# One wide expert body with the choice of passes inside its blocks, first gates ahead of the dispatch, both tiles scattered by the next expert

## The reference, cut to what matters

```python
logits = (h @ w_router).astype(jnp.float32)
top_vals, top_idx = lax.top_k(logits, TOP_K)
gates = jax.nn.softmax(top_vals, axis=-1)
...
for e in range(N_EXPERTS):
    # swiglu: gu = h @ w_gu[e]; (silu(gu[..., :FF]) * gu[..., FF:]) @ w_down[e]
    y = y + comb[..., e:e + 1] * swiglu(h, w_gu[e], w_down[e])
return rmsnorm(h + y, final_norm_g)
```

## Time and profile before

| | |
|---|---|
| median of 3 runs | 1764.01 us (1763.48 to 1765.18) |
| the profiled execution | 1751.77 us, of which the span is 1750.0 us |
| granted TensorE clock, mean | 0.970 |
| busy share of the span: TensorE / its weight loads / VectorE / ScalarE / GpSimd | 93% / 75% / 72% / 58% / 7% |
| chain that ended last, by engine | PE 69%, DVE 11%, DMA 11%, ACT 4%, issue 4% |

### The profile page before, as it was taken

The page is one execution under the profiler, slowest core; times in us unless marked ns, Lnnn a source line. Parts: engine busy times, 40 slices in busy tenths (PEclk is TensorE's granted clock), DMA queues, the critical chain, the costliest instruction groups (busy, mean ns, idle before and its releaser), DMA issues.

```text
span 1750.0 us, 20830 instructions
## 1 busy us (share of the span) xinstructions
PE 1621.6 (93%) x7345; PEld 1318.3 (75%) x7346; DVE 1257.8 (72%) x1028; ACT 1022.6 (58%) x872; POOL 120.9 (7%) x90
## 2 busy tenths in 40 slices
PE   7999999999899769999999999999999599899996
PEld 5887778888788657777778878778888377677775
DVE  6745554544579559999988888655554499899996
ACT  4344344344348337887877777544443378788874
POOL 0000000000000003030030030020000030200300
PEclk9999999999999869999999999999999799999998
DMA  9652545555542118999999989846565299999994
GB/s 356 200 194 96 181 159 190 192 180 193 174 151 73 48 50 330 394 391 389 395 361 382 344 328 368 298 168 204 204 210 198 84 347 396 341 388 395 379 395 180
DMA packets 191591, 450.82 MB, mean 258 GB/s; under 512 B 8492, under 2 KB 8892, under 8 KB 191420
## 3 DMA queue, kind: packets, MB, share of 16 engines
q1 hardware_dynamic: 189212, 445.35, 70.2%
q10 hardware_dynamic: 2336, 4.85, 0.8%
HBM read 449.13 MB, written 1.05 MB: 257 GB/s over the span
## 4 chain that ended last, share of the span: by engine, by line
PE 69%; DVE 11%; DMA 11%; ACT 4%; issue 4%; SPq 0%; DVEq 0%; ACTq 0%; POOL 0%; POOLq 0%
PE bank L1148 19%; PE bank L1149 18%; PE bank L1152 18%; DMA raw<-in_moe_w_down 10%; DVE wlo L701 6%; ACT whi L406 4%; PE bank L1155 3%; PE bank L1156 3%; DVE y L939 2%; PE bank L1426 1%; PE bank L1425 1%; PE bank L1323 1%; PE bank L1325 1%; PE bank L1441 1%; PE bank L1442 1%
## 5 line engine op out<-in xcount | busy, mean ns | idle before, releaser
L701 DVE TENSOR_TENSOR wlo<-raw,whi 128x2048 fp32r<-128x2048 f32 x422 | 963.3, 2292 | 301.5 <-ACT whi L406 300.3
L406 ACT ACTIVATE whi<-raw 128x2048 fp32r<-128x2048 f32 x422 | 805.1, 1915 | 426.3 <-PE bank L1152 343.9
L1148 PE MATMUL bank<-whi,xx 128*128 128x512 f32 x1184 | 473.8, 400 | 47.3 <-issue 22.9
L1149 PE MATMUL bank<-wlo,xx 128*128 128x512 f32 x1184 | 466.0, 394 | 0.0
L1152 PE MATMUL bank<-whi,xx 128*128 128x512 f32 x1184 | 465.7, 393 | 0.0
L1148 PEld LDWEIGHTS bank<-whi,xx 128*128 128x128 f32 x1184 | 225.5, 190 | 97.3 <-issue 30.3
L1152 PEld LDWEIGHTS bank<-whi,xx 128*128 128x128 f32 x1184 | 225.3, 190 | 48.4
L1149 PEld LDWEIGHTS bank<-wlo,xx 128*128 128x128 f32 x1184 | 226.0, 191 | 45.3
L375 POOL TENSOR_SCALAR onehot<-mats,slot 128x64 fp32r<-128x64 f32 x64 | 110.3, 1747 | 921.6 <-PE bank L1432 921.6
L1155 PE MATMUL bank<-whi,hT 128*128 128x512 f32 x336 | 138.7, 413 | 23.8 <-DVE wlo L701 23.2
L1155 PE MATMUL bank<-whi,xx 128*128 128x512 f32 x336 | 133.6, 398 | 0.2
(11 more groups left out here) (201 smaller groups left out, 1298.6 us busy)
## 6 DMA issues: line engine op xcount, KB each, us to landing
raw<-in_moe_w_gu SPq DMA_DIRECT2D x224, 1024.0 KB, 7.7
raw<-in_moe_w_down SPq DMA_DIRECT2D x112, 1024.0 KB, 8.1
raw<-in_ffn_w_gu SPq DMA_DIRECT2D x28, 1024.0 KB, 5.0
raw<-in_ret_w_in SPq DMA_DIRECT2D x24, 1024.0 KB, 6.0
raw<-in_ffn_w_down SPq DMA_DIRECT2D x14, 1024.0 KB, 4.7
raw<-in_conv_w_pw SPq DMA_DIRECT2D x12, 1024.0 KB, 5.1
raw<-in_ret_w_out SPq DMA_DIRECT2D x8, 1024.0 KB, 4.7
res<-in_x SPq DMA_DIRECT2D x2, 512.0 KB, 5.3
```

Of the source, the lines that this page charges most:

```text
L406: nc.scalar.activation(whi[base % SPLIT][:, :], raw[base % RAW][:, :], ACT.Copy).then_inc(hi_done, 1)
L701: nc.vector.tensor_tensor(wlo[base % SPLIT][:, :], raw[base % RAW][:, :], whi[base % SPLIT][:, :].bitcast(f32), ALU.subtract).then_inc(lo_ ...
L1148: nc.tensor.matmul(dst, ah, bh, start=start, stop=False)
L1149: last = nc.tensor.matmul(dst, ah, bl, start=False, stop=stop and al is None)
```

## The change

- **Dispatch.** TensorE's loop computes tile 0's first two gate blocks ahead of the branch (`gates_first(0)`). The bodies are laid out as kind 0, kind 1, and one wide body for kinds 2 and 3; the four static ones become three.
- **Choice inside the wide body.** Each up block, down block and transposition does tile 0, and then branches on `need > 2` for tile 1: 35 such choices in a wide expert (2 + 1 ahead of the loop, 5 in each of 6 iterations, 2 behind it).
- **`pe_done`** of the first two gate blocks is raised by 2 at once: in a narrow body by a matmul of four columns with zeros (`nothing`) behind the branch, in the wide body behind tile 1's gates.
- **Wide entry.** Tile 0's gates no longer wait for tile 1: it has its own `xel2_done`. The order is gates of tile 0, branch, gather of tile 1, scatter of the previous expert, gates of tile 1. ScalarE's `hi` of the second block moves ahead of `xh_gathered2`, VectorE's `xl_gathered2` behind `y_lo`.
- **Wide exit.** The body's own scatter, `accumulate2` and both waits go. The next expert's `scatter_before` (in all three bodies and behind the loop) reads the previous expert's need and scatters one tile or two into the same banks, so that one `accumulate` adds both.

```diff
-            dve.wait_ge(moe_set, 4)
+            dve.wait_ge(moe_set, 5)
...
-            def xl_gathered(e, tiles, n):
+            def xl_gathered(e):
...
+            def xl_gathered2(n):
+                dve.wait_ge(xeh2_done, n + 1)
...
+                last.then_inc(xel2_done, 1)
...
-                xl_gathered(e, tiles, n2)
+                xl_gathered(e)
                 lo(B_MOE + 1, six)
                 y_lo(e)
+                if tiles == 2:
+                    xl_gathered2(n2)
...
                 if tiles == 2:
                     y_lo2(n2)
-                    accumulate2(e, n2)
...
+            def nothing(dst):
+                return nc.tensor.matmul(dst[:, 0:4], zeros[:, 0:P], zeros[:, 0:4], start=False, stop=True)
+
+            def expert_columns(base, acc, half, kind, need, six):
                 pe.wait_ge(lo_done, base + 1 + 6 * six)
+                if kind == WIDE:
+                    chunk_columns(base, acc[0], half, 0, FULL)
+                    with pe.If(need > 2):
+                        chunk_columns(base, acc[1], half, 1, FULL).then_inc(pe_done, 1)
+                    with pe.Else():
+                        chunk_columns(base, acc[1], half, 1, HALF_FULL).then_inc(pe_done, 1)
+                else:
+                    chunk_columns(base, acc[0], half, 0, kind).then_inc(pe_done, 1)
...
+            def scatter(tiles):
+                for t in range(TILES):
+                    for s in range(tiles):
...
+            def scatter_before(e):
+                pe.wait_ge(yl_done, e + 1)
+                with pe.If(need_before(pe, e) > 1):
+                    pe.wait_ge(y2l_done, wide_before(pe, e))
+                    scatter(2)
+                with pe.Else():
+                    scatter(1)
...
-            def expert(e, kinds):
...
-                pe.wait_ge(xel_done, e + 1)
-                columns(B_MOE, bank[0:2], 0, kinds=gates, six=six)
-                columns(B_MOE + 1, bank[0:2], 1, kinds=gates, six=six)
-                pe.wait_ge(yl_done, e + 1)
-                scatter(0, SCAT).then_inc(scat_ps, 1)
+            def expert(e, kind, need):
+                six, done, tiles = STEPS * e, STEPS * e + STEPS, 2 if kind == WIDE else 1
+                gates_end = nothing(bank[0])
+                if kind == WIDE:
+                    gather(e, 1).then_inc(gather2_ps, 1)
+                    scatter_before(e)
+                    pe.wait_ge(xel2_done, wide_before(pe, e) + 1)
+                    gates_first(1, six).then_inc(pe_done, 2)
+                else:
+                    gates_end.then_inc(pe_done, 2)
+                    scatter_before(e)
...
-                if tiles == 2:
-                    pe.wait_ge(y2l_done, n2 + 1)
-                    scatter(1, SCAT2).then_inc(scat2_ps, 1)
-                    pe.wait_ge(acc2_done, n2 + 1)
...
                 need = need_of(pe, e)
+                pe.wait_ge(xel_done, e + 1)
+                gates_first(0, STEPS * e)
+                with pe.If(need < 1):
+                    expert(e, HALF_FULL, need)
+                with pe.Else():
+                    with pe.If(need < 2):
+                        expert(e, FULL, need)
                     with pe.Else():
+                        expert(e, WIDE, need)
-            pe.wait_ge(yl_done, NE + 1)
-            scatter(0, SCAT).then_inc(scat_ps, 1)
+            scatter_before(NE)
```

More of the change, by code:

```diff
@@ L36 @@
 PAD = TAPS - 1
-FULL, HALF_FULL = 1, 2
+FULL, HALF_FULL, WIDE = 1, 2, 3
 MOE_BLOCKS = STEPS * STEP_BLOCKS
@@ new lines, in chunk_rows @@
+            def chunk_rows(base, first_chunk, stop, t, kind):
+                slot_ = base % SPLIT
+                for c in range(2):
+                    kc = first_chunk + c
+                    for n in range(2):
+                        col = c * D + n * BANK
+                        wh, wl = whi[slot_][:, col:col + BANK], wlo[slot_][:, col:col + BANK]
+                        dst = DOWN[t][n][:, :]
+                        if kind == HALF_FULL:
+                            last = half_product(dst, hTmix[:, kc, t, :], wh, wl, False, stop and c == 1)
+                        else:
+                            last = product(dst, hTh[:, kc, t, :], hTl[:, kc, t, :], wh, wl, False, stop and c == 1)
+                return last
@@ new lines, in scatter, with gates_first @@
+                last.then_inc(scat_ps, 1)
+            def scatter_before(e):
[3 more added lines that the diff above has]
+                    scatter(2)
+                with pe.Else():
+                    scatter(1)
+            def gates_first(tile, six):
+                for half in range(2):
+                    pe.wait_ge(lo_done, B_MOE + half + 1 + 6 * six)
+                    slot_ = (B_MOE + half) % SPLIT
+                    for c in range(4):
+                        kc = 4 * half + c
+                        last = product(bank[tile][:, :], xh[:, kc, tile, :], xl[:, kc, tile, :],
+                                       whi[slot_][:, c * BANK:(c + 1) * BANK], wlo[slot_][:, c * BANK:(c + 1) * BANK],
+                                       kc == 0, tile == 1 and kc == DC - 1)
+                return last
```

167 lines of the change are left out of this document (77 added, 90 removed).

## The result

The changed kernel takes **1737.48 us** (median of 4 runs, 1735.81 to 1740.53), beside 1763.74 us for the kernel before (4 runs): ratio 0.9854, interval 0.9842 to 0.9867. It gained 26.3 us; 10.9 were forecast, and 1753 us.

The account below looks back on a forecast made before the run. VectorE was taken to pace kind-0 stretches and TensorE the wide one, with code fetches at boundaries. Terms summed to -10.9 us, -16 of it at the wide exit: 1764.0 to 1753 us, range 1742 to 1763.

Parts of the forecast that it names:

- the same step: From profiled execution to median: the 12.2 us by which the median lay above it carried over unchanged, giving 1753 us.
- Leaving the wide expert: Wide expert's end to the next `hidden`: wait, scatter and `accumulate2` removed, fetch covered; -16 us (bounds -17 and -11).
- Expert 6: Start after the wide expert: its existing fetch stall stays, 0; -5.6 us if the smaller program stays at hand.
- Where a body ends: Start of expert 1: jump to the loop's end, code that never ran, costs a fetch; +5.6 us (bounds 0 and 5.6).
- Expert 3: Late `pe_done` there is hidden, since the chain ends where TensorE's up blocks end anyway: 0.
- `pe_done` late: Narrow experts: block 3's split waits for the late signal, delaying `hidden`; +1.2 us each for experts 1, 6 and 7.
- Wide entry: Entering the wide expert: full-clock gates and no fetch, but a new wait before the scatter; -3.5 us (bounds -6.3 and 0).
- The choices: The 35 branches in the wide body: 0.03 us each, +1 us in all (bounds 0 and 5).
- Expert 0: Its gates can start when `xx` is ready, partly offset by late `pe_done` and clock; -2.6 us (bounds -2.6 and 0).
- The first: Rival: all code stays at hand, no fetch at the starts of experts 1 and 6; 1742 us, chance 0.26.
- The second: Rival: late `pe_done` and body fetches at several narrow starts take the gain back; around 1764 us, chance 0.12.
- The third: Rival: the choices in the wide body drain TensorE, 0.6 us each; 1773 us, slower, chance 0.10.

Follow-up runs that it names:

- fourth look: One more profiled execution of the kernel before, unchanged: 1764.33 us.
- first look: The profiled execution of the kernel before, unchanged, on which the prediction was made: 1751.77 us.
- own_scatter: The changed kernel, but the wide expert again scatters its own tile 1 and waits, and `scatter_before` reads no table: 1740.01 us.
- narrow_first: The kernel before with only its four bodies reordered to kind 0, 1, 3, 2: 1753.4 us, ratio 0.9952.
- wide_first: The changed kernel with the wide body first, then kind 1 and kind 0: 1743.48 us.
- gates_in_bodies: The changed kernel with the first gates back in the bodies and `pe_done` raised by each block: 1743.36 us.
- one_narrow: The changed kernel with its two narrow bodies merged into one that chooses between the passes of kinds 0 and 1 inside its blocks: 1749.94 us.
- hinted: early_inc plus a branch hint on the back-edge of TensorE's expert loop: 1733.24 us, ratio 0.9837.
- early_inc: The changed kernel with `pe_done` raised once behind the first gate block of narrow experts: 1737.81 us.
- wide_first_hinted: wide_first plus the early `pe_done` increment in narrow experts and the hint on TensorE's expert loop back-edge: 1736.53 us.
- one_narrow_hinted: one_narrow plus the early `pe_done` increment in narrow experts and the hint on TensorE's expert loop back-edge: 1748.19 us.

## Why the prediction was wrong

**The step that failed** is the last: "The median is 12.2 above that execution; the same step puts the prediction at" 1753. It carries the offset over as if the change couldn't touch it. After has none (1737.84 profiled, 1737.48 median). The 26.3 us are 13.9 between the profiles, 12.0 of before's offset (1763.74 - 1751.77), and 0.4 of after's. Most of the offset (8.1 us by the fourth look) was late code at experts 5 to 7, with the clock behind it, and after has no such stall at 6 and 7; the rest was clock in an uncommonly fast first look. The sum itself, -10.9, missed the 13.9 by only 3, and that is partly luck: expert 6 came out 5.5 us shorter than forecast, and expert 3 came out 3.1 us longer. The fourth look is the execution to compare with; against it, after's stretches differ by -3.1 (up to expert 0), +6.8 (1), -0.2 (2), +1.5 (3), -4.8 (4), -17.5 (5), -5.5 (6), -4.4 (7) and +0.5 at the end: -26.5. Beside the forecast of -10.9, experts 6 and 7 make up 12.3 of the 15.6 us that are missing (+1.2 was forecast for each).

**Leaving the wide expert.** Forecast -16, between the profiles -16.2, and in the parts foreseen: input 6.4 us after the last product (1373.01 + 1.28 against 1367.85; 6.6 forecast), gates 6.6 after it, no fetch in the open. I had priced the whole, and not how it splits; 12.3 of it came in *own_scatter*, without moving the scatter.

**Expert 6.** This is the term of the sum that failed. I kept its stall at 0, with -5.6 as a bound "if the smaller program stays at hand". It went: -4.3 between the profiles, -5.5 with the late `pe_done` in it against the fourth look. With expert 7's stall, unseen in the first profile, that is the unforeseen part.

**Where a body ends.** Expert 1: forecast 5.6 + 1.2, measured 6.77, and *narrow_first* shows the cause alone (6.7 there without the late `pe_done`, and with more time at the low clock, so the match to a tenth is luck). **Expert 3**: forecast 0, measured +3.1. It jumps to the loop's end as expert 1 does, and I had that fetched once and for all. In *wide_first* the stall is gone with the order. Its stretch is 1.6 us longer than before's all the same, but before's own fourth look has that too (127.9), by the clock.

**`pe_done` late**: forecast 1.2, measured 1.3 at expert 7 and 1.1 by *gates_in_bodies*.

**Wide entry**: forecast -3.5, measured -3.0. The gather follows the gates without a gap, as foreseen. The wait is 4.49 us and not 3.9, and ends in "issue" 1.1 us after `yl` (1147.03 + 1.29): no instruction packet moves in it. It is the table read and the branch of `scatter_before`: *own_scatter*, which has neither, waits 3.48 us, and `yl` releases it. So an "issue" ending alone doesn't show a late instruction stream, and expert 0 showed the reverse, late code under another name; the packets have to be looked at. The read was left out of the sum here and put at +1 for the last scatter, where the wait did grow from 2.50 to 3.47 us; the last stretch, whose clock varies, went from 117.76 to only 117.87. The term of 2.8 for the clock has no row: the gates of the earlier trace rows take 7.5 instead of 5.5 us, which is 2.0.

**The choices**: forecast +1, measured 0 in the wide loop. **Expert 0**: forecast -2.6, measured -1.2 between the profiles, or -2.0 from the stage's own start, which came 0.8 us later. The size is near, the reason isn't: what stood before the gates was the fetch of the body. In *narrow_first*, with the gates in the body and the kind-0 body right behind the dispatch, it is gone; in *wide_first*, with the gates ahead and the wide body behind the dispatch, it stands behind the gates (2.45 and 2.91 us).

**The rivals.** The first, with all code at hand at 1742, was nearest in time, but not what happened: expert 1 stalls, expert 6 doesn't. The second was right in that one more narrow start stalls (expert 3), and wrong at the exit (-16.2, not -11) and at the wide entry (-3.0, not 0). The third fell with the step of the wide loop, 30.47 to 30.49 us with and without choices.

**Size or order.** Size alone doesn't rank the kernels: 1,660 instructions took 1750 us, 1,550 took 1725.5, and 1,840 took 1737.5 or, in another order, 1743.5. With the other edits and the body order left as before, it does: 2,360, 1,780 and 1,550 instructions give 1763, 1737.5 and 1725.5 us. The Trainium skill's page "Runtime: NRT & Kernel Launch", section "Instruction fetch mechanics", gives TensorE 128 KiB in blocks of 256 instructions; an estimate by it puts *one_narrow*'s stage at 104 KiB, all of it at hand once run, and the trace with its fetch at expert 2 disagrees. Which blocks are kept, and so where a layout stalls, no run here settles. One rival is untested: every edit that changes size or order also shifts where the code lies within its blocks, and no run shifted it alone.

## What to carry to other kernels

Code of a branchy stage is a resource: merging two bodies by a branch inside their blocks took 21 to 23 us off without touching the executed work, because a boundary that jumps to code not at hand costs 2 to 5.3 us of idle TensorE in these traces and 2 to 7.5 us of time, and a chain of such jumps left a gap of 19 to 21 us where 6.4 remain with the code at hand. Moving bodies mostly moves the stalls, and the result of a layout has to be measured. Before a sum is made on one profile, look at a second and third execution: where they differ from each other by a stall, that part of the median's offset belongs to that kernel and may vanish with the change. And look at the instruction packets beside a gap, since the releaser that the profile names can be wrong in both directions.

## What the runs showed that I had not expected

- The same program, on the same data, has two or three late starts in experts 5 to 7: 1751.8, 1756.5, 1760.9 and 1764.3 us in four profiled executions of before.
- After the same wait of 1.54 us the granted clock was 1.00 in one execution and 0.54 in another, which alone made expert 3's stretch 1.5 us longer.
- Branches to code at hand are free in a stretch that TensorE bounds (30.47 to 30.49 us a step with five and with none), and cost about 1 us in a kind-0 stretch of *one_narrow*, which VectorE paces. Reading a word of the table and branching on it, between a wait and the first matmul, cost 1.0 us (4.49 against 3.48, and 3.47 against 2.50).
- A smaller program (1,660 against 1,840 instructions) fetched code again that had already run, and was 12 us slower.
- A hint on one back-edge went with 4.6 us less in *hinted* (against *early_inc*, intervals overlapping) and, together with the early increment, with 7.0 us less in *wide_first_hinted* and nothing measurable in *one_narrow_hinted* (1748.19 against 1749.94).
